# Modulation weights in 64-row tiles, two column blocks side by side

## The reference

```python
c_act = jax.nn.silu(c)
mod = jnp.dot(c_act, ada_w[l]) + ada_b[l]
sh1, sc1, g1, sh2, sc2, g2 = jnp.split(mod, N_MOD, axis=-1)
h = modulate(rms_norm_2(x, norm1_g[l]), sh1, sc1)
...
x = x + g1[:, None, :] * jnp.einsum('bsd,de->bse', merged, w_out[l])
h = modulate(rms_norm_2(x, norm2_g[l]), sh2, sc2)
```

## Time and profile before

| | us |
|---|---|
| median of 3 runs | 890.72 |
| lowest and highest | 890.26, 891.99 |
| profiled execution, device time | 891.36 |
| span in its trace | 890.0 |

### The profile page before, as it was taken

How to read it: one execution, slowest core, us unless ns; L and a number is a source line. 1 busy time by engine, 2 the same in 40 slices (tenths; PEclk the granted TensorE clock), 3 DMA queues, 4 the chain that set the end, 5 groups by cost and what they waited for, 6 DMA issues and landing times.

```text
span 890.0 us, 18499 instructions
## 1 busy us (share of the span) xinstructions
PE 879.5 (99%) x7364; PEld 856.3 (96%) x7364; DVE 731.0 (82%) x1168; ACT 569.9 (64%) x836; POOL 1.9 (0%) x9
## 2 busy tenths in 40 slices
PE   8999999999999999999999999999999999999997
PEld 7999989999999999999999999889999999999996
DVE  6778999899998899898965999998788885555554
ACT  7838456775586787664446868667785664444542
POOL 0000000000000000000000000000000000000000
PEclk9999999999999999999999999999999999999998
DMA  8866456556875789999856566753545666666651
GB/s 313 268 188 224 150 152 210 164 177 213 295 258 182 266 290 343 352 334 312 335 177 204 167 202 197 200 161 130 168 142 188 191 193 203 194 193 193 185 166 48
DMA packets 54549, 189.83 MB, mean 213 GB/s; under 512 B 6192, under 2 KB 8640, under 8 KB 54336
## 3 DMA queue, kind: packets, MB, share of 16 engines
q1 hardware_dynamic: 54320, 188.65, 64.5%
q10 hardware_dynamic: 144, 0.00, 0.0%
HBM read 186.53 MB, written 1.05 MB: 211 GB/s over the span
## 4 chain that ended last, share of the span: by engine, by line
PE 90%; ACT 4%; DVE 4%; issue 1%; DMA 1%; SPq 0%; DVEq 0%; ACTq 0%
PE bank L1020 27%; PE bank L1022 27%; PE bank L1023 27%; PE bank L995 1%; PE bank L994 1%; PE bank L993 1%; ACT whi L1957 1%; DVE wlo L1064 1%; DMA H<-in_xT 1%; PE bank L729 1%; PE bank L965 0%; PE bank L972 0%; PE bank L968 0%; DVE mqk L1487 0%; PE bank L831 0%
## 5 line engine op out<-in xcount | busy, mean ns | idle before, releaser
L1957 ACT ACTIVATE whi<-raw 128x1024 fp32r<-128x1024 f32 x297 | 311.7, 1057 | 190.4 <-PE bank L1023 180.7
L1064 DVE TENSOR_TENSOR wlo<-raw,whi 128x1024 fp32r<-128x1024 f32 x297 | 360.3, 1220 | 88.7 <-ACT whi L1957 88.1
L1020 PE MATMUL bank<-Alo,whi 128*128 128x256 f32 x1344 | 376.1, 280 | 0.0
L1022 PE MATMUL bank<-Ahi,wlo 128*128 128x256 f32 x1344 | 372.1, 277 | 0.0
L1023 PE MATMUL bank<-Ahi,whi 128*128 128x256 f32 x1344 | 372.1, 277 | 0.0
L1020 PEld LDWEIGHTS bank<-Alo,whi 128*128 128x128 f32 x1344 | 252.6, 188 | 2.8 <-issue 2.6
L1022 PEld LDWEIGHTS bank<-Ahi,wlo 128*128 128x128 f32 x1344 | 252.6, 188 | 0.4 <-issue 0.2
L1023 PEld LDWEIGHTS bank<-Ahi,whi 128*128 128x128 f32 x1344 | 252.7, 188 | 0.0
L1022 PE MATMUL bank<-Fhi,wlo 128*128 128x256 f32 (+1 forms) x320 | 88.8, 277 | 0.0
L1023 PE MATMUL bank<-Fhi,whi 128*128 128x256 f32 (+1 forms) x320 | 88.8, 277 | 0.0
L1020 PE MATMUL bank<-Flo,whi 128*128 128x256 f32 x256 | 70.9, 277 | 0.0
(11 more groups left out here) (421 smaller groups left out, 1371.1 us busy)
## 6 DMA issues: line engine op xcount, KB each, us to landing
raw<-in_stream SPq DMA_DIRECT2D x298, 512.0 KB, 4.4
araw<-in_ada SPq DMA_DIRECT2D x48, 512.0 KB, 6.0
TB<-in_TB SPq DMA_DIRECT2D x1, 1536.0 KB, 7.5
a8r<-a SPq DMA_DIRECT2D x16, 64.0 KB, 3.7
out<-H SPq DMA_DIRECT2D x4, 256.0 KB, 2.9
bc<-in_bc SPq DMA_DIRECT2D x1, 896.0 KB, 8.5
H<-in_xT SPq DMA_DIRECT2D x1, 512.0 KB, 7.4
mats<-in_mats SPq DMA_DIRECT2D x1, 449.0 KB, 7.2
```

The costliest lines, as they stand in the source:

```text
L1020: pe.matmul(os[j], wh, xl, start=k == 0 and (wide or j == 0), stop=False, skip_group_check=not wide)
L1022: pe.matmul(os[j], wl, xh, start=False, stop=False, skip_group_check=not wide)
L1064: v.tensor_tensor(wlo[:, s % NHL, :], raw[:, s % NRAW, :], whi[:, s % NHL, :].bitcast(F32), ALU.subtract).then_inc(*lo_v.up(s))
L1957: a.activation(whi[:, s % NHL, :], raw[:, s % NRAW, :], ACT.Copy).then_inc(*hi.up(s))
```

## The change

The eight groups of 128 rows and six blocks of 1024 columns become sixteen groups of 64 rows and three pairs of blocks. A tile holds 64 rows of one block on partitions 0 to 63 and the same 64 rows of the next block on partitions 64 to 127. It is still 128x1024, there are still 48, and a row of it is still 4 KB in memory, but it takes two transfers of 64 partitions instead of one of 128. An accumulator gathers sixteen tiles and covers two blocks. The transposes of an accumulator give, in each 128 columns of the bank, 64 values of the one block and 64 of the other, and VectorE reduces the halves apart: four reduces of 128x256 per sum instead of two of 128x512. There are three sums, after tiles 15, 31 and 47. `csil` becomes a tile of its own, 128x16, in the place of an unused one, filled by four small transfers of 64x8 at the start, behind slab 6; it holds SiLU(c) of each 64 rows in both halves of the partitions.

```diff
-SUMS = [ADA[8 * b + 7] + 2 for b in range(6)]
+SUMS = [ADA[16 * b + 15] + 2 for b in range(3)]
...
-    "sums": (SUMS, [n + 1 for n in SUMS] + [SUMS[5] + 3], []),
+    "sums": (SUMS, [n + 1 for n in SUMS] + [SUMS[2] + 3], []),
...
-        sb("gap0", [128, 16])
+        csil = sb("csil", [128, 16])
...
-                    sp.dma_start(araw[:, n % 3, :], A["ada"][n % 8, :, (n // 8) * 1024:(n // 8) * 1024 + 1024]
-                                 ).then_inc(*ar_in[n % 3].up(n, by=16))
+                    r, c0 = n % 16, (n // 16) * 2048
+                    for h in range(2):
+                        sp.dma_start(araw[64 * h:64 * h + 64, n % 3, :],
+                                     A["ada"][r // 2, r % 2 * 64:r % 2 * 64 + 64, c0 + 1024 * h:c0 + 1024 * h + 1024]
+                                     ).then_inc(*ar_in[n % 3].up(n, by=16))
...
             load_slab(6)
+            for h in range(2):
+                for b in range(2):
+                    sp.dma_start(csil[64 * h:64 * h + 64, 8 * b:8 * b + 8],
+                                 A["cols"][64 * b:64 * b + 64, COFF["c"]:COFF["c"] + 8]).then_inc(*c_in.up("in", by=16))
...
             def sums():
-                for cb in range(6):
+                for cb in range(3):
                     w.wait_ge(*mats_in.at("in"))
-                    w.wait_ge(*ada_v.at(8 * cb + 7))
+                    w.wait_ge(*ada_v.at(16 * cb + 15))
...
-                for cb in range(6):
-                    for k in range(8):
-                        n, o = 8 * cb + k, aacc[cb % 2][:, :]
+                for cb in range(3):
+                    for k in range(16):
+                        n, o, at = 16 * cb + k, aacc[cb % 2][:, :], 8 * (k % 2) + k // 2
...
-                            v.tensor_scalar(o, araw[:, n % 3, :], csil[:, k:k + 1], None, ALU.mult).then_inc(*ada_v.up(n))
+                            v.tensor_scalar(o, araw[:, n % 3, :], csil[:, at:at + 1], None, ALU.mult).then_inc(*ada_v.up(n))
...
                     for j in range(2):
-                        i = v.tensor_reduce(mod[:, 8 * cb + 4 * j:8 * cb + 4 * j + 4],
-                                            banks[6 + j][:, :].rearrange("p (a c) -> p a c", a=4), AXX, ALU.add)
+                        for h in range(2):
+                            at = 8 * (2 * cb + h) + 4 * j
+                            i = v.tensor_reduce(mod[:, at:at + 4],
+                                                banks[6 + j][:, :].rearrange("p (a h c) -> p a h c", a=4, h=2)[:, :, h, :],
+                                                AXX, ALU.add)
...
-                w.wait_ge(*red_v.at(5))
+                w.wait_ge(*red_v.at(2))
...
-                a.activation(csil[:, :], cols[:, COFF["c"]:COFF["c"] + 8], ACT.Silu).then_inc(*ada_s.up("c"))
+                w.wait_ge(*c_in.at("in"))
+                a.activation(csil[:, :], csil[:, :], ACT.Silu).then_inc(*ada_s.up("c"))
```

More of the change, by code:

```diff
@@ L373, in build @@
         ang, kf, pT = ple[:, 2, :], ple[:, 3, :], ple[:, 4:6, :]
-        g2, csil = modg[:, 16:24], shb
+        g2 = modg[:, 16:24]
         aacc = (aacc0, aacc1)
@@ L450, in build @@
         ar_in = signals("ar0 ar1 ar2")
-        g1_in, cols_in, mats_in, bc1_in, sgw_in, wa2_in, tb_in, pos_in, pT_in, bc2_in, stored = signals(
-            "g1 cols_l mats_l bc1_l sgw_l wa2_l tb_l pos_l pT_l bc2_l stored")
+        g1_in, c_in, cols_in, mats_in, bc1_in, sgw_in, wa2_in, tb_in, pos_in, pT_in, bc2_in, stored = signals(
+            "g1 c_l cols_l mats_l bc1_l sgw_l wa2_l tb_l pos_l pT_l bc2_l stored")
         hi, lo_v, mm, drained_s, drained_v = signals("hi lo_v mm drained_s drained_v")
@@ L1008, in tensor_program @@
                         os = [b[:, 0:T + 2], banks[second][:, 0:T + 2]]
-                        w.wait_ge(*(red_v.at(5) if name == "mq0" else root.at("r3") if name == "mq1"
+                        w.wait_ge(*(red_v.at(2) if name == "mq0" else root.at("r3") if name == "mq1"
                                     else ml_s.at("root", 1, 1)))
@@ L1387, in ada @@
                                 w.wait_ge(*mm.at("wo", 3))
-                            v.tensor_scalar(o, araw[:, n % 3, :], csil[:, k:k + 1], None, ALU.mult).then_inc(*ada_v.up(n))
+                            v.tensor_scalar(o, araw[:, n % 3, :], csil[:, at:at + 1], None, ALU.mult).then_inc(*ada_v.up(n))
                         else:
                             w.wait_ge(*ada_v.at(n - 1))
-                            v.scalar_tensor_tensor(out=o, in0=araw[:, n % 3, :], scalar=csil[:, k:k + 1], in1=o,
+                            v.scalar_tensor_tensor(out=o, in0=araw[:, n % 3, :], scalar=csil[:, at:at + 1], in1=o,
                                                    op0=ALU.mult, op1=ALU.add).then_inc(*ada_v.up(n))
```

## The result

The changed kernel takes 947.29 us (938.76 to 952.07, 4 runs) where the kernel before takes 891.36 in the same measurement: 1.062 times as long, 95% interval 1.058 to 1.065. The forecast was 887.4 with a range to 904.0, so sign and size are wrong. Run again beside other kernels, the changed one took 950.10 (943.84 to 953.20).

A forecast was written before the change was run, and what follows sets the result against it. TensorE, busy 99%, was taken to bound the kernel; three fewer sums save 3.3 us and every other term counts nothing, so 890.72 becomes 887.4 us. Own range 886.3 to 888.9, widened up to 904.

The forecast's parts named there:

- Three sums fewer: On TensorE: each sum costs 1.11 us, so three fewer save 3.3 us on the path that sets the end.
- a sum worth less than counted: On TensorE: filler hides, only 0.87 us of transposes go per sum; 2.6 us saved, 888.1; chance within the forecast's 0.58.
- Reduces, tile steps: On VectorE: twelve reduces shrink from 681 to 412 ns, 3.2 us off the path; 48 tile steps unchanged; both count nothing.
- The start: Four small transfers behind slab 6 make slab 7 and its followers 0.6 us late, up to 1.4 us; counted as nothing.
- The cover: At TensorE's first products on the normed input: 2.7 us of slack against 1.4 us of lateness.
- Twice as many issues: On SyncE: 48 more issues of 0.33 us, 16 us spread over 220 us; queue has room, counted as nothing.
- The shape of the transfers: Modulation tiles in 302 to 442 us: two 64-partition transfers each; from zero cost to half the rate, taken near zero.
- f: Factor on modulation tiles' 56.4 us of DMA time in 302 to 442; taken near 1, upper bound 2.
- rival 1: DMA engines become the bound in 302 to 442 us: 899.3 at f = 1.5, 927.5 at f = 2; chance 0.31.
- The 5.1 us of lead: In 302 to 442 us: ScalarE's slab copies run 5.1 us ahead of TensorE, covering that much DMA shortfall.
- The estimate of 903.8: Skill page's rates give f = 328/208 = 1.58, a 21.5 us shortfall in 302 to 442, less cover and gain.
- Rival 2: VectorE lagging in 342 to 362 us, or the start shift, takes the TensorE gain back: 889 to 892; chance 0.11.

The follow-up runs named there:

- halves alone: The kernel before with slabs 230 to 297 loaded as two transfers of 64 partitions each, modulation tiles whole: 891.95 us, ratio 1.0007.
- the two queues: The kernel before with each modulation tile in halves, the lower issued by SyncE and the upper by ScalarE: 943.04 us, ratio 1.057.
- the first experiment: The kernel before with each modulation tile loaded as two transfers, partitions 0 to 63 and 64 to 127, six sums, old order: 943.23 us, ratio 1.061.

## Why the prediction was wrong

**Three sums fewer: right.** 1.11 us forecast for each, 1.10 in the changed kernel, and 3.2 and 3.3 us saved in the two versions of the change whose transfers are not slow (888.38 against 891.58; 888.55 against 891.84). The rival of a sum worth less than counted falls with it.

**Reduces, tile steps: right.** 412 ns as forecast, and VectorE's busy total is 730.2 us against 731.0.

**The start: right in what it costs.** SyncE's timeline of the changed kernel has the four small transfers and the slab behind them:

```profile
12.08 0.33 SPq L502 DMA_DIRECT2D raw<-in_stream  x1
12.46 2.48 SPq L551 DMA_DIRECT2D csil<-in_cols  x4
15.04 13.85 SPq L502 DMA_DIRECT2D raw<-in_stream  x8
```

From slab 6 to slab 7 it is 2.96 us instead of 2.17, so 0.8 us where I had 0.6. The cover held: the version with whole transfers has the same start and its full gain.

**Twice as many issues: right in what they cost.** An issue of 64 partitions took 0.59 us (median of 96), not the 0.33 I had. The run with every second partition has the same median and as many issues, and loses nothing.

**The shape of the transfers: the step that failed.** I wrote "So I take f near 1" because a half microsecond of rotations among slabs showed 352 GB/s at 0.92, and set aside the row beside it, 232 GB/s per unit of share. Measured f was 2.03 to 2.33, worked out below. The first row was a window of 0.5 us, and from it I could not know how many of its bytes were of which kind. The 2.25 us right behind it in the same trace, with rotations and a slab still in flight, show the opposite:

```profile
574.75:577.00 2.25, 2.25 (x16) 1.49 (x17) 2.25 (x12) 0.45 (x2) 0.00 (x0) 1.00 0.99 231
```

That row alone speaks against f near 1. The second row, 232, lies close to the 236 of halves alone, but that may be luck: the rotations copy 32 partitions to 32 others in tiles that already lie on the chip, in rows of 2 KB, and no run shows that they are slow for the same reason. Nor does the argument hold that engines apart in time write different halves so that f = 2 is hardly reached: it was reached with one queue and with two.

The working of rival 1 was right in place and mechanism (share at 1.0, slabs late, TensorE short of low parts), and its size is the rest of the miss: 947.29 lies 19.8 us over its worst case. In the stage's terms, DMA-busy time is 72.4 us for slabs and 56.4f for tiles. Halves alone say f = 359/236 = 1.52, and 1.27 with pauses. With every tile in halves it is 46.2 MB at 250 GB/s and share 1.01, so 186.7 us, f = 2.03, my upper bound; in the changed kernel it is 198 x 1.03 = 203.9 us, f = 2.33, beyond it. So 927.5 us, the worst that I priced, was passed: a tile in halves in this stage costs more DMA time than twice a whole one, counting what it does to others. So f is not the price of the tiles alone: the two queues above show whole slabs at 236 GB/s per unit of share beside halves, as slow as these, where I had left the slabs' 72.4 us unchanged. How the slabs' later landing (13.4 us instead of 5.9) divides into moving slower and waiting in the queue stays open, and so does what in the path of a transfer makes it slow. Every other tile in halves gave 163.3 x 1.01 - 72.4 - 28.2 = 64.3 us for the halved 28.2, f = 2.3; so the price of a halved tile does not grow with their number. The 5.1 us of lead as cover fits that run (20.6 us lost, 20 expected).

It fits the first experiment too. Between its first and its last sum that lost 48.1 - 6.4 = 41.7 us, and 186.7 - 140 - 5.1 gives 41.6. The whole loss was 51.7. The other 10 us are 6.4 before the first sum, 1.7 behind the last, and 2.2 by which the median lies above the profiled execution, less 0.2 for the same difference in the kernel before. The 6.4 belong to the first eight tiles, which I had left out. They are not the same in every execution: with two queues the first sum is only 0.7 us late (263.1), and TensorE's busy time in 213 to 302 of the changed kernel is 1.2 us short of 89:

```profile
213.00:302.00 89.00, 87.79 (x759) 86.89 (x759) 80.07 (x114) 60.91 (x88) 0.00 (x0) 1.00 0.89 244
```

**The Trainium skill against the row.** Its page "SBUF — State Buffer" gives 328 GB/s for all partitions and 196 for a half (section "Door 1: The DMA port swizzle"), and 6% more for two at once (section "Can I just issue two DMAs to hit both halves?"). From these came my estimate of 208 and a factor of 1.58. Halves alone measured 1.52 here in a burst, near it, and 1.27 over a stretch with pauses. The estimate of 903.8 made from it missed 947.29 as well, since it priced the tiles and not what they do to the slabs beside them.

**Rival 2** (gain taken back by VectorE or the start) did not happen: in the version with whole transfers the stage runs without a TensorE wait.

## What to carry to other kernels

When a transfer is cut, look at which partitions each piece reaches, not at how many: here pieces that stayed in one half of the array cost 1.3 to 1.5 times the DMA time by themselves and 2.0 to 2.3 times beside whole transfers, and pieces that interleave (every second partition) cost nothing. Before taking such a cut as free, compare the stage's share of DMA time with 1: at 0.63 the same cut was invisible, at 0.92 it cost 6%. And when two rows disagree about the only open price, widen the windows before choosing: the 0.5 us that the forecast rested on were followed by 2.25 us with a third less.

## What the runs showed of the hardware

Transfers of 64 partitions in one half stream 236 GB/s at a full share. Mixed with whole ones the DMA moves 230 to 250 GB/s in 302 to 442, hardly more than halves by themselves, although 56% of the bytes go in whole transfers: these slow down with the halves (236 GB/s per unit of share in the queue of the slabs, 361 before). With half of a tile's rows in such transfers it is 283 and 284. Transfers to every second partition did not show it (368 GB/s at 0.99), and by its time neither did one across the middle of the array.

The granted TensorE clock of the changed kernel is a mean of 0.91 in 302 to 442, a mixture of its levels of 2.4 and 1.2 GHz. It was 1.00 in 302 to 322, with TensorE busy for 19.77 of 20 us, 0.91 in 342 to 362 with 17.07, but 1.00 again in 442 to 462 with only 16.59. Since the DMA engines were at a share of 1.03 all through that stage, I take it that the clock set no time there; no run shows it by itself. Before the first sum of the first experiment it can be part of the 6.4 us: there a TensorE wait of 2.96 us ends at 264.35, and in 255 to 270 the clock was 0.89 with the DMA at a share of only 0.87.
